# Decoder trunk on one core: 16 activation tiles computed around the gate maps and kept in memory, residual adds placed among the last rows, first queries split by tokens

## The reference

```python
def peer_mixer(h, wq, subkeys, u, v):
    q = (h @ wq).reshape(B, S, 8, 2, 128)
    scores = jnp.einsum('bshcd,hcnd->bshcn', q, subkeys)
    s_top, i_top = lax.top_k(scores, 16)
    ...                                   # 16x16 sums of both halves, top 16: expert_idx, gates
    u_sel = jnp.take(u, ii, axis=0)
    a = jnp.einsum('cd,ced->ce', hh, u_sel)
    act = jax.nn.gelu(a, approximate=False) * gg
    return jnp.einsum('ce,ced->cd', act, jnp.take(v, ii, axis=0))
```

## Time and profile before

| | |
|---|---|
| median of 3 runs | 3720.78 us (3720.15 to 3722.91) |
| the profiled execution | 3715.07 us, of which the span is 3713.3 us |
| busy in the span | PE 3447.6, DVE 2581.6, POOL 1356.5, ACT 987.9 us |
| read from memory, written | 971.85 MB, 25.17 MB |

### The profile page before, as it was taken

One profiled execution on the slowest core, in us unless ns is written; L12 is line 12 of the kernel. 1 busy time (PEld: TensorE's weight loads), 2 busy tenths in 40 slices (PEclk: granted clock), 3 DMA queues, 4 the chain that ended last, 5 costly groups with the idle time before them and its releaser, 6 DMA issues.

```text
span 3713.3 us, 46396 instructions
## 1 busy us (share of the span) xinstructions
PE 3447.6 (93%) x13798; PEld 2206.2 (59%) x13798; DVE 2581.6 (70%) x5509; ACT 987.9 (27%) x2173; POOL 1356.5 (37%) x1220
## 2 busy tenths in 40 slices
PE   6999998999948999999989999989996599999998
PEld 4555445777745458884445544467766544688643
DVE  5766016988898777876576731288998977787766
ACT  2433112323354003330023330122333720133200
POOL 0000002554423666666500000044544146666662
PEclk8999999999989999999989999999998999999999
DMA  5432215888756999999953312178887489999998
GB/s 224 174 107 85 91 64 214 327 318 330 278 186 238 405 401 398 368 381 393 409 213 108 130 74 101 59 276 334 327 303 286 147 323 405 409 390 373 392 402 326
DMA packets 275134, 999.40 MB, mean 269 GB/s; under 512 B 31481, under 2 KB 48377, under 8 KB 264449
## 3 DMA queue, kind: packets, MB, share of 16 engines
q0 software_dynamic: 153600, 553.72, 38.9%
q1 hardware_dynamic: 121346, 443.42, 31.8%
HBM read 971.85 MB, written 25.17 MB: 268 GB/s over the span
## 4 chain that ended last, share of the span: by engine, by line
PE 48%; DVE 18%; DMA 15%; issue 9%; POOL 4%; DVEq 3%; ACT 2%; ACTq 0%; POOLq 0%; SPq 0%
PE ps L585 10%; PE ps L857 9%; DMA arena<-in_u_dram,idx 8%; PE ps L632 6%; DMA arena<-in_v_dram,idx 5%; PE ps L552 4%; PE ps L543 4%; PE ps L653 3%; DVE arena L1512 3%; POOL arena L1255 3%; DVE mod L1518 3%; PE ps L575 2%; PE ps L520 2%; PE ps L676 2%; DVE mod L1532 1%
## 5 line engine op out<-in xcount | busy, mean ns | idle before, releaser
L1255 POOL DMA_INDIRECT arena<-in_u_dram,idx x512 | 668.6, 1306 | 1016.8 <-issue 396.2
L585 PE MATMUL ps<-hT,mod 128*128 128x256 f32 x4096 | 925.9, 379 | 0.0
L632 PE MATMUL ps<-arena 128*128 128x512 f32 x1984 | 852.8, 593 | 4.3 <-DVE arena L1543 3.4
L585 PEld LDWEIGHTS ps<-hT,mod 128*128 128x128 f32 x4096 | 759.3, 190 | 92.1
L1255 POOL DMA_INDIRECT arena<-in_v_dram,idx x512 | 590.9, 1154 | 597.4 <-DVE mod L1518 293.2
L1512 DVE CUSTOM_DVE_ANT_0 arena<-arena 128x1024 f32<-128x1024 f32 x512 | 618.1, 1224 | 242.1 <-DMA arena<-in_u_dram,idx 239.0
L1518 DVE SCALAR_TENSOR_TENSOR mod<-arena,mod 128x1024 f32<-128x1024 f32 x512 | 657.4, 1284 | 155.0 <-DMA arena<-in_v_dram,idx 123.2
L632 PEld LDWEIGHTS ps<-arena 128*128 128x128 f32 x1984 | 377.1, 190 | 477.5 <-issue 470.7
L1056 ACT COPY mod<-ps 128x512 f32<-128x512 f32 x512 | 274.4, 590 | 505.0 <-PE ps L575 505.0
L575 PE MATMUL ps<-const,arena 128*128 128x128 f32 x2048 | 266.1, 273 | 6.4 <-ACT mod L1056 5.4
L575 PEld LDWEIGHTS ps<-const,arena 128*128 128x128 f32 x2048 | 237.4, 141 | 36.9 <-issue 13.3
(11 more groups left out here) (214 smaller groups left out, 3541.5 us busy)
## 6 DMA issues: line engine op xcount, KB each, us to landing
arena<-in_u_dram SPq DMA_DIRECT2D x256, 512.0 KB, 7.0
arena<-in_v_dram SPq DMA_DIRECT2D x256, 512.0 KB, 6.9
arena<-in_ada_w_dram SPq DMA_DIRECT2D x56, 1024.0 KB, 5.6
arena<-in_w_qkv_dram SPq DMA_DIRECT2D x48, 512.0 KB, 7.1
arena<-in_w_m_dram SPq DMA_DIRECT2D x16, 1536.0 KB, 6.2
arena<-in_w_q_dram SPq DMA_DIRECT2D x32, 576.0 KB, 6.9
gate_scratch<-hT SPq DMA_DIRECT2D x64, 256.0 KB, 2.1
hT<-gate_scratch POOLq DMA_DIRECT2D x128, 128.0 KB, 8.0
```

The source lines that it names most:

```text
L585: last = pe.matmul(ps[:, 6 + tile // 2 % 2, tile % 2 * NT:(tile % 2 + 1) * NT], u_turned[:, tile % 2, k * P:(k + 1) * P], hT[:, k, DT0:SEQ ...
L632: last = pe.matmul(ps[:, 2 * c + n, :], act_t[:, e, c * P:(c + 1) * P], stream[:, slot, n * 512:(n + 1) * 512], start=(half == 0 and e == ...
L1255: pool.indirect_dma_start(out=ring[:, r % RING, :], out_offset=None, in_=table, in_offset=bass.IndirectOffsetOnAxis(ap=idx[:, j % 4, k:k + ...
```

## The change

- **Activation tiles 0 to 15 of the second half** are computed early: PE does tiles 0 to 3 ahead of the gate maps' first batch and tiles 4 to 15 one by one after batches 2, 5, 7, 10, 13, 15, 18, 21, 23, 26, 29 and 31. Their turned u goes to two free buffers, their results to two staging buffers, which SP writes to memory (8 writes of 256 KB); four reads of 512 KB bring them back during the first half's value tiles. Later only 48 tiles are left between the two value stages. Value tiles start when tile 15 too is done. SP's queue in the maps holds these loads, the gates' writes and the tiles' writes in one order.
- KEEP0 and KEEP1 move from 368 and 432 to 328 and 392; `kept_maps` waits for the four reads.
- **At the end** `add_to_x` is split: chunk 0 is added and normed after row 495, chunks 2 and 3 after row 503, chunk 1 after row 511. x is read back after the last value tile was requested, not among them.
- **At the head**, chunk 2 is transposed before PE's last product with w_out; head 0's query is made for tokens 0 to 383 before chunk 3's transposes and for 384 to 511 after them; DVE does rows 0 to 15 before it waits for the scores, and rows to 158 before `gates_dense`. The first u tile is turned earlier.

The core of the diff; the rest renames, counts the loads' semaphores anew and picks the other buffers:

```diff
+QUERY_BANK = 6
 KEPT = 4
+EARLY = 16
+FIRST = 4
+EARLY_AT = [-1] * FIRST + [b for b in range(NB) if (EARLY - FIRST) * (b + 1) // NB > (EARLY - FIRST) * b // NB]
+BACK = 4
+LATE_UNIT = 9
+LATE_GATES = [22, 38, 56]
...
-KEEP0 = 16 * 23
-KEEP1 = 16 * 27
+KEEP0 = 328
+KEEP1 = 392
+LAST_ROWS = UNITS * ROWS - TOPK
+KEY = 256.0
+ORDER = [[0, 1, 2, 3], [0, 2, 3, 1]]
...
+        u_early = [mod[:, GAIN2, :], g_row[:, :]]
+        staged = [part(A_STAGED, 2 * NT), x[:, 0, 0:2 * NT]]
...
+        def tiles_at(b):
+            return [t for t in range(EARLY) if EARLY_AT[t] == b]
...
+                def early_u():
+
+                    for t in range(STREAM):
+                        after_u(HALF - STREAM + t)
+                        load_u(l * TILES + HALF + t, t)
+
+                def during_maps():
+
+                    for b in range(-1, NB):
+                        for t in tiles_at(b):
+                            if t == 0:
+                                after_u(HALF)
+                                load_u(l * TILES + HALF + STREAM, 0)
+                            if t + 1 < EARLY:
+                                after_u(HALF + t + 1)
+                                n = t + 1 + STREAM
+                                if n < EARLY:
+                                    load_u(l * TILES + HALF + n, n % STREAM)
+                                else:
+                                    load_v(l * TILES + n - EARLY, n % STREAM)
+                        if b >= 0 and b % 2 == 1:
+                            for r in (b - 1, b):
+                                sp.wait_ge(S["gs_done"], NB * l + r + 3)
+                                park()
+                                sp.dma_start(gate_dram[:, r:r + 1, :].rearrange("p a (b n) -> p (a b) n", b=2),
+                                             kept[r % KEPT]).then_inc(kept_out[r % KEPT], 16)
+                        for t in tiles_at(b):
+                            if t % 2 == 1:
+                                q = t // 2
+                                sp.wait_ge(S["a_ev"], HALF * l + HALF // 2 + q + 3)
+                                park()
+                                sp.dma_start(act_dram[:, 2 * q:2 * q + 2, :],
+                                             staged[q % 2].rearrange("p (a n) -> p a n", a=2)).then_inc(act_out[q % 2], 16)
+
+                def acts_back():
+
+                    for i in range(2):
+                        sp.wait_ge(act_out[i], 16 * (EARLY // 4) * (l + 1))
+                        park()
+
+                def more_v(half, first, end):
+                    with sp.Fori(first, end) as r:
+                        for s in range(STREAM):
+                            tile = l * TILES + HALF * half + STREAM * r + s
+                            sp.wait_ge(S["st_used"], tile + 1)
+                            park()
+                            load_v(tile, s)
+
+                def first_v():
+                    more_v(0, 1, 10)
+                    acts_back()
+                    for g in range(EARLY // BACK):
+                        sp.dma_start(act_t[:, BACK * g:BACK * (g + 1), :],
+                                     act_dram[:, BACK * g:BACK * (g + 1), :]).then_inc(S["act_back"], 16)
+                        more_v(0, 10 + g, 11 + g)
...
+                    more_v(1, 5, 14)
                     if l + 1 < DEPTH:
                         load_g(l + 1, 0)
                     else:
                         sp.wait_ge(S["norm_gain"], 2 * DEPTH + 1)
                         sp.dma_start(g_row[:, :], io["final_g"].partition_broadcast(P)).then_inc(S["g_in"], 16)
-                    more_v(14, HALF // STREAM)
+                    more_v(1, 14, HALF // STREAM)
+                    sp.wait_ge(S["topk_done"], UNITS * l + UNITS)
+                    for ch in ORDER[1]:
+                        sp.dma_start(x[:, ch, :], x_dram[:, ch, :]).then_inc(S["x_back"], 16)
...
-                with pe.Fori(0, NB // 2) as g:
-                    for s in range(2):
-                        b = NB * l + 2 * g + s
-                        pe.wait_ge(S["p_done"], b + 1)
-                        pe.wait_ge(S["q_done"], b + 1)
-                        pe.wait_ge(S["gm_done"], b + 1)
-                        pe.wait_ge(S["gs_done"], b + 1)
-                        for t in range(BATCH):
-                            last = pe.matmul(ps[:, G_BANK[s] + t // 4, t % 4 * P:(t % 4 + 1) * P],
-                                             p1[:, s, t * P:(t + 1) * P], q1[s][:, t * P:(t + 1) * P], start=True, stop=True)
-                        last.then_inc(S["g_done"], 1)
+                pe.wait_ge(S["qst_ev"], 2 * HEADS * (l + 1) + 2)
+                pe.wait_ge(S["sc_ev"], 2 * HEADS * (l + 1) + 2)
+                turn_u(l, 1, 0)
+                act_tiles(l, 1, 0, FIRST, EARLY)
+                for b in range(NB):
+                    s = b % 2
+                    pe.wait_ge(S["p_done"], NB * l + b + 1)
+                    pe.wait_ge(S["q_done"], NB * l + b + 1)
+                    pe.wait_ge(S["gm_done"], NB * l + b + 1)
+                    pe.wait_ge(S["gs_done"], NB * l + b + 1)
+                    for t in range(BATCH):
+                        last = pe.matmul(ps[:, G_BANK[s] + t // 4, t % 4 * P:(t % 4 + 1) * P],
+                                         p1[:, s, t * P:(t + 1) * P], q1[s][:, t * P:(t + 1) * P], start=True, stop=True)
+                    last.then_inc(S["g_done"], 1)
+                    for t in tiles_at(b):
+                        act_tiles(l, 1, t, t + 1, EARLY)
...
+                    pe.wait_ge(S["a_ev"], HALF * l + HALF // 2 + EARLY // 2 + 2)
...
+                transposes(l, 1, 2, h2)
                 out_rows(l, 3, 1)
-                transposes(l, 1, 2, h2)
+                pe.wait_ge(S["sc0_ev"], 2 * l + 2)
+                park()
+                pe.wait_ge(S["hT_ev"], 4 * CH * l + 2 * CH + 6)
+                park()
+                for c in range(2):
+                    query_of(l, 0, c, QUERY_BANK + c, slice(0, 3 * P))
                 transposes(l, 1, 3, h2)
+                turn_u(l, 0, 0)
                 pe.wait_ge(S["hT_ev"], 4 * CH * l + 4 * CH)
                 park()
-                pe.wait_ge(S["sc0_ev"], 2 * l + 2)
-                park()
+                for c in range(2):
+                    query_of(l, 0, c, QUERY_BANK + c, slice(3 * P, SEQ)).then_inc(S["query_done"], 1)
                 for hd in range(HEADS):
-                    query(l, hd, 0)
-                    query(l, hd, 1)
+                    if hd > 0:
+                        query(l, hd, 0)
+                        query(l, hd, 1)
                     head_scores(l, hd)
-                    if hd == 0:
-                        turn_u(l, 0, 0)
                     if hd < HEADS - 1:
-                        act_tiles(l, 0, ENDS[hd], ENDS[hd + 1])
-                act_tiles(l, 0, ENDS[-1], HALF)
+                        act_tiles(l, 0, ENDS[hd], ENDS[hd + 1], HALF)
+                act_tiles(l, 0, ENDS[-1], HALF, HALF)
                 turn_picks(l)
                 gate_maps(l)
                 value_tiles(l, 0)
-                turn_u(l, 1, 0)
-                act_tiles(l, 1, 0, HALF)
+                turn_u(l, 1, EARLY)
+                act_tiles(l, 1, EARLY, HALF, HALF)
...
+                early = half == 1 and 2 * pair < EARLY
+                to = staged[pair % 2] if early else act_t[:, 2 * pair:2 * pair + 2, :].rearrange("p a n -> p (a n)")
+                if early and pair >= 2:
+                    act.wait_ge(act_out[pair % 2], 16 * (EARLY // 4) * l + 16 * (pair // 2))
+                act.activation(to, ps[:, (2 if early else 6) + pair % 2, :], ACT.Gelu).then_inc(S["a_ev"], 1)
...
-                for b in range(NB):
-                    p_batch(l, b)
+                u_out(l, 1, 0)
+                for b in range(NB + 1):
+                    if b < NB:
+                        p_batch(l, b)
+                    for t in tiles_at(b - 1):
+                        act_tile(l, 1, t, EARLY)
                     if b >= 1:
                         keep_batch(l, b - 1)
-                keep_batch(l, NB - 1)
-                for j in range(5, 9):
+                for j in range(5, LATE_UNIT):
                     unit_gates(l, j)
-                u_out(l, 1, 0)
-                for tile in range(HALF):
-                    if tile in (4, 19, 33, 48):
-                        unit_gates(l, 9 + (4, 19, 33, 48).index(tile))
-                    act_tile(l, 1, tile)
-                for j in range(13, UNITS):
+                u_out(l, 1, EARLY)
+                for tile in range(EARLY, HALF):
+                    if tile in LATE_GATES:
+                        unit_gates(l, LATE_UNIT + LATE_GATES.index(tile))
+                    act_tile(l, 1, tile, HALF)
+                for j in range(LATE_UNIT + len(LATE_GATES), UNITS):
...
+                if part == 0:
+                    dve.wait_ge(S["act_back"], 16 * (EARLY // BACK) * (l + 1))
```

(36 more changed lines are left out.)

160 lines of the change are left out of this document (86 added, 74 removed).

## The result

| | before | after |
|---|---|---|
| median of 4 runs each, in turns on one chip | 3721.85 us (3720.15 to 3731.29) | 3788.36 us (3779.49 to 3802.74) |
| ratio | | 1.0175, 95% interval 1.0152 to 1.0197 |
| profiled execution (span) | 3715.1 us (3713.3) | 3779.5 us (3777.8) |

The changed kernel is slower by 66.5 us. The forecast was 3736 us, and the range ended at 3762. Between the two profiled executions lie 64.4 us where the sum had 15.4.

A forecast was written before the change was run, and what follows sets the result against it. Several limits, by stage: DVE in the gate maps, PE and full DMA queues side by side behind them. Layers +2.5 and +12.9, together +15.4 on 3715.1, gave 3730.5; the median lies 5.7 higher, so 3736 us, range 3686 to 3762.

The forecast's parts named there:

- The head: Stretch before the gate maps: PE's first query and DVE's moved rows shorten waits, -5.1 + 1.7 = -3.4 us a layer.
- the six moved rows at 1.2 us each: Before the scores: DVE does six more rows at 1.2 us each, and its 7.0 us wait there is gone.
- The upper bound of +3: Worst case before the maps: the early tiles' loads delay the rows there, +3 us a layer.
- The gate maps: Between first and last batch: 12 steps of 6.35 us and 19 of 2.9, 131 us; +15.3 and +18.1 by layer.
- From the last batch on: Last batch to next projection or end: PE, remaining rows, additions and closing work; -9.4 us in layer 0, -1.8 in layer 1.
- 51 + 21: After PE's end in layer 0: 51 us for 35 remaining rows plus 21 us of DVE for three chunks' adds and norms.
- The 1.45: Rows left after PE's end go at POOL's pace, 1154 ns and 0.3, 1.45 us a row.
- the 2.0 us a row: Rows after PE's end if VectorE kept GpSimd from writing descriptors: 2.0 us each, adding 19 us a layer; left open.
- The first: Rival behind the maps: tiles hide, rows keep pace with bytes, fewer than about 15 rows left; 3686 us, chance 0.2.
- The second: Rival in the gate maps: their slack pays for the tiles, 0 instead of 15 and 18; 3703 us, chance 0.17.
- The third: Rival in the gate maps: tiles wholly exposed, by ACT's order or a lower clock, +37 and +34 more; 3807 us, chance 0.07.
- The clock: First batches of the maps: PE's filled pause avoids the lower clock, saving 1 or 2 us a layer; left out of the sum.

## Why the prediction was wrong, step by step

**The head (-3.4, measured +16.1 and +12.1) is the step that failed.** I had both halves of the mechanism: that row 16's gather would have no cover, and that PE starts its tiles earlier. But I counted PE's earlier start as a gain alone. It also starts the u stream 10 us earlier, while the gathers of rows 8 to 15, which the moved rows now call for before the top-k, are on the same queues. I had looked at the DMA share of the stages behind the maps and not at that of the head: the earlier trace rows starts at 1036. The term that was wrong is the six moved rows at 1.2 us each: rows 8 to 14 took 2.6, and row 15 came 30.2 us behind row 0, where it came at 19.3 with the query whole. The upper bound of +3 came from "the early tiles' loads", the wrong transfer. Nothing in my range stood for two edits that are harmless singly. (A slip without weight: the earlier trace rows has 5.2 for the second wait where the sum has 5.1.)

**The gate maps (+15.3 and +18.1, measured +18.9 and +22.7): mechanism right, size short.** The steps behind a tile are 6.2 us as forecast at 6.35, but three of them in layer 0 and four in layer 1 take some 7.8, with PE at the lower clock in part; the steps without a tile average 3.1 and not 2.9. The kernel before had slow batches too: in its layer 0 the batches 23 to 26 took 2.61, 3.76, 2.64 and 3.64 us, which helps make its maps 118.0 there and 115.2 in layer 1. Against 115.2 the change cost 21.7 in layer 0. There are 11 tile steps, not 12: the last tile stands behind the last batch. First value tile 4.7 us after the last batch (forecast 4.6).

**From the last batch on (-9.4 and -1.8, measured -6.1 and +0.7): near term by term, one of them by luck.** PE 656.2 us where I had 651.4. The 4.8 us were to be seen beforehand: the same prices per tile give 716 us for the kernel before, whose trace has 721.1 from the first value tile to PE's end, and I compared my sum with that kernel's measured time. Rows left at its end 35 and 34, forecast 35. From there to the last row 70.5 us in layer 0 (forecast 51 + 21 = 72): 20.0 of it are the three chunks, so a row takes 50.5 / 35 = 1.44 us, forecast 1.45. Last row to projection 10.9, to the end 9.9 (11 and 10). Of the 3.3 us missing in layer 0 PE's 4.8 are the cause, less the 1.5 that the rows made good.

The 1.45 had the wrong reason, though. I took it as POOL's pace. But DVE waits only 1.5 us for gathers in this stretch, and its rows take 1.37 us each even at the very end, where the last eight gathers had all been issued by 1894.22, 11 us before DVE took the first of these rows:

```profile
1851.19 21.94 DVE L1632 SCALAR_TENSOR_TENSOR mod<-arena,mod 128x1024 f32<-128x1024 f32 x16
...
1894.22 0.94 POOL L1369 DMA_INDIRECT arena<-in_v_dram,idx  x1 [0.30 <-issue]
...
1905.23 10.92 DVE L1632 SCALAR_TENSOR_TENSOR mod<-arena,mod 128x1024 f32<-128x1024 f32 x8
```

21.94 / 16 and 10.92 / 8 are both 1.37: DVE's own rate from row to row is this and not the 1.28 of one operation. POOL issued the gathers beside the first sixteen at the same 1.37 us (1.07 and 0.3), so the two could not be told apart there. The Trainium skill's page SBUF — State Buffer, two separate sides, says that a VectorE operation in a two-port mode keeps GpSimd from writing descriptors. No run here shows that the rows' operations, which read two inputs, are in one, so these runs neither bear the rule out nor refute it; the 2.0 us a row that I priced beside it did not come.

**The rivals.** The first (few rows left, additions hide) is ruled out for sixteen tiles by the 35 rows left, but its threshold of 15 rows was good: with four tiles 8 or 9 rows are left and the additions give their 10 us. The second (the slack pays for the tiles) falls at sixteen tiles and holds for most of the cost where three stand among the maps, 1.4 us each for 4.33 of work. The third is ruled out by the steps.

**The clock.** I left 1 to 2 us a layer for the filled pause out of the sum. In layer 0 0.7 of it came: the first batch took 3.08 us instead of 3.75, though PE had idled only 2.57 us before it, and the second 2.56 as before (2.51). In layer 1 1.7 came: 2.02 instead of 3.75, after 1.71 us of idle time. It came with PE's lateness and not with the filled pause alone: with both parts of the head taken back, PE idled 4.8 and 4.9 us between these tiles and the first batch, and the batch took 3.75 both times. The lines are those of layer 0.

```profile
1052.54 3.08 PE L703 MATMUL ps<-cos_sin,mod 128*128 128x128 f32 x16 [2.57 <-issue]
1055.42 2.56 PE L703 MATMUL ps<-arena,mod 128*128 128x128 f32 x16
```

## What to carry to other kernels

An engine that starts earlier also starts its loads earlier: before crediting a head start, read the DMA share of that very stretch and ask which transfers it will stand beside, and what the queues will find to do after it. Two edits that each move a wait can meet in one place; cost them together, and undo them one at a time and both at once when the sum is off. Where two chains end together, relief for one is worth what the other allows: here 70 us of PE work a layer were moved, and from the last batch on the end came 6 us sooner in one layer and no sooner in the other.

## What the runs showed of the hardware

- A stretch of full DMA queues was not made up later: 24 us at 1.02 and 399 to 409 GB/s were followed by 24 us at 0.31 and 0.16, since the gathers that could have used them had no indices yet (POOL waited 35.32 us for them).
- Beside the u stream rows 10 to 15 came every 2.2 us in layer 0, with half of the stream left out every 1.7, and every 1.3 with the query whole, where the stream begins 10 us later.
- TensorE fell to the lower clock in the middle of the maps after idle gaps of a few microseconds. In the window of the slow batch and tile above the granted clock is 0.81, in the next 1.00; the batch took 2.52 us for 1.95, the eight transposes 1.91 for 1.04. That made this step 1.6 us longer than its like, and there are three such in layer 0 and four in layer 1. The gap alone does not decide it: after the same 2.7 us of idle time the 22nd batch took 2.02 us in layer 0 and 2.89 in layer 1.

```profile
1094.00:1103.00 9.00, 6.71 (x35) 6.39 (x36) 9.00 (x21) 5.37 (x13) 2.25 (x2) 0.81 0.53 160
1103.00:1112.00 9.00, 6.77 (x53) 6.24 (x52) 5.59 (x13) 7.07 (x19) 0.00 (x0) 1.00 0.52 160
```

- Stays open: why the profiled executions of equal heads differ by up to 9 us (434 to 443 from row 0 to the maps); DVE's waits for gathers at rows 17 to 21 and before the maps differ among them, and no run here tells what they depend on.
